# Every fourth expert slot of the first tile summed by POOL in SBUF instead of by PE

## The chip, the cores and the metric

The kernel runs on one core of a Trainium2 chip. The number is the device time of one execution in microseconds; the median of three runs of the kernel before is 1160.29 us (1155.86 to 1161.13). All arithmetic is in float32.

## The reference, cut to what matters

Two transformer blocks over 256 tokens of width 1024. The change touches one part of the second, the expert layer. For each token, 8 heads choose 16 of 16,384 experts each, so 128 experts a token. An expert is a row of `u` and a row of `v`, 1024 numbers each.

```
act = gelu(einsum('thkd,td->thk', u[expert], xt))      # one dot product a chosen expert
return einsum('thk,thkd->td', w * act, v[expert])      # weighted sum of the 128 rows of v
...
h = h + peer_ffn(rmsnorm_2(h, ffn_norm), ...)
gate = sigmoid(rmsnorm_2(h, ple_gate_norm) @ ple_gate_w)
h = h + (p @ ple_proj) * gate
```

## The kernel before

The 256 tokens are two tiles of 128, a token a partition. A slot is one chosen expert of every token of a tile: slots 0 to 127 belong to tile 0, 128 to 255 to tile 1. The expert part works slot after slot, and its order is written out by hand in the program of each engine.

POOL issues one gather a slot (L511). It brings 128 rows of 8 KB, the `u` and the `v` row of each token's expert, into a page of SBUF. Pages are old buffers under their old names: `ig`, `kT`, `spare`, `tail`, `xc_rg`, `gl`, `ga`, and from slot 35 on also `sm`. So there are seven pages for slots 0 to 27 and eight later, and a gather waits until the slot that had the page before is done (`slot_before`). The seventh slot before slot 10 is slot 3; slot 22 takes the page of 15, slot 30 that of 23.

DVE makes the dot product of the `u` half with the token's row (`dot`, L2038) and writes one number a token. Between dots it goes on choosing the experts of later heads, two steps a slot for 10 of 16 slots. ACT takes two slots at a time (`weigh`): gelu (L1406), times the probability (L1412), then for each slot a diagonal matrix of the weights (L1420, four buffers). PE multiplies that diagonal with the `v` half, 2 x 512 columns, and so adds the weighted rows to the sums in PSUM (`expert_sum`, L973). These sums started from the residual. When PE is done with a slot it raises `row_used`, for which POOL's gather waits.

In the first 52 slots of tile 0, PE, ACT and DVE also finish the attention and the mixing of tile 1's tokens between the slots (`second_tokens`; scores L721, turned weights L730, values L743, queries L922); DVE's L1750 and L1753 belong to it. From slot 52 on PE makes tile 1's queries. When tile 0's slots are summed, ACT copies the sums to `x3` (`tile_sums`, L1426), DVE makes their squares (L2045), PE turns them (L1074), DVE multiplies by a gain (`norm_out`, L1527), PE makes the gate (L1082), one product behind each slot of tile 1 (`first_gate`), and DVE adds the gated part (L2060). SP loads the weights of later stages into a ring of three slots.

Of the kernel before, what the change touches and what calls it, by code (L numbers as in the profile page):

```python
# [19 lines left out]
ALU = mybir.AluOpType  # L20
# [5 lines left out]
D = 1024  # L26
NT = SEQ // P
KC = D // P
HALF = 512
# [67 lines left out]
for _name, _width in COLS:  # L97
# [16 lines left out]
        "mixT_made", "mixed_full", "sums_copied", "sums_turned", "sums_gained", "rstd_made", "wp_used", "wo_full", "keys_loaded", "tok_full", "tok_moved", "query_turned", "query_moved",  # L114
        "pscore_full", "pscore_moved", "ple_moved",
        "choice_step", "top_shift", "top_exp", "chosen", "prob_made", "dot_made", "gelu_made", "w_made", "diag_made",
        "row_used", "sums_moved", "h2_made", "gate_full", "gate_moved", "y_made"]

# [2 lines left out]
BATCH = 2  # L123
DIAGS = 4
LAG = 32
TILE_SLOTS = PEER_HEADS * TOPK
SLOTS = NT * TILE_SLOTS
# [24 lines left out]
def slot_before(g):  # L152

    n = landing_of(g)
    return PAGE_SLOTS[page_of(g)][n - 2] if n > 1 else None

# [26 lines left out]
def two_blocks(nc, x, wall, cols, rows, lambdas, sub_keys, peer_uv, out):  # L185
    with ExitStack() as ctx:
# [231 lines left out]
        def _(pool):  # L418
# [76 lines left out]

            pool.wait_ge(s["intra_masked"], 2)

            for g in range(SLOTS):
                if g % TOPK == 0:
                    pool.wait_ge(s["chosen"], g // TOPK + 1)  # L500
                if g == 4:

                    pool.wait_ge(s["o_full"], NT)
                if g == 6:
                    pool.wait_ge(s["o_gated"], NT)
                if g == PAGE_SLOTS[7][0]:

                    pool.wait_ge(s["ao_full"], len(STEPS2))
                if slot_before(g) is not None:
                    pool.wait_ge(s["row_used"], slot_before(g) + 1)  # L510
                nc.gpsimd.indirect_dma_start(out=rows_uv[page_of(g)], out_offset=None, in_=peer_uv,  # L511
                                             in_offset=bass.IndirectOffsetOnAxis(ap=experts[:, g:g + 1], axis=0))\
                    .then_inc(row_here[page_of(g)], 16)
# [3 lines left out]
        def _(pe):  # L517
# [449 lines left out]
            att_turn(2)  # L967

            def expert_sum(g):
                t, n = g // TILE_SLOTS, g % DIAGS  # L970
                pe.wait_ge(s["diag_made"], g + 1)
                for c in range(2):
                    ins = nc.tensor.matmul(acc[t][:, c, :], diag[:, n * P:(n + 1) * P],  # L973
                                           rows_uv[page_of(g)][:, D + c * HALF:D + (c + 1) * HALF],
                                           start=False, stop=True, skip_group_check=True)
                ins.then_inc(s["row_used"], 1)
# [109 lines left out]

            def first_gate():

                for _ in range(4):
                    yield  # L1090
                pe.wait_ge(s["ple_moved"], 2)
                turn_sums(0)
                for _ in range(4):
                    yield
                pe.wait_ge(s["normed"], 2 * NT + 1)
                for c in range(2):
                    for k in range(KC):
                        embedding_gate(0, c, (k,))
                        yield

            for g in range(TILE_SLOTS):
                expert_sum(g)
                second_tokens(g)
            between = first_gate()
            for g in range(TILE_SLOTS, SLOTS):
# [9 lines left out]
        def _(act):  # L1115
# [285 lines left out]
            def weigh(b):  # L1401

                slots = range(b * BATCH, (b + 1) * BATCH)
                at = slots[0] % LAG
                act.wait_ge(s["dot_made"], slots[-1] + 1)
                nc.scalar.activation(acts[:, at:at + BATCH], dots[:, at:at + BATCH], ACT.Gelu_apprx_tanh)\  # L1406
                    .then_inc(s["gelu_made"], 1)
                if slots[0] % TOPK == 0:
                    act.wait_ge(s["prob_made"], slots[0] // TOPK + 1)
                act.wait_ge(s["gelu_made"], b + 1)  # L1410
                for g in slots:
                    ins = nc.scalar.activation(wk[:, g % LAG:g % LAG + 1], acts[:, g % LAG:g % LAG + 1], ACT.Copy,  # L1412
                                               scale=probs[:, g:g + 1])
                ins.then_inc(s["w_made"], 1)
                act.wait_ge(s["w_made"], b + 1)
                for g in slots:
                    if g >= DIAGS:
                        act.wait_ge(s["row_used"], g - DIAGS + 1)
                    n = g % DIAGS
                    nc.scalar.activation(diag[:, n * P:(n + 1) * P], ident[:, :], ACT.Copy,  # L1420
                                         scale=wk[:, g % LAG:g % LAG + 1]).then_inc(s["diag_made"], 1)

            def tile_sums(t):

                act.wait_ge(s["row_used"], (t + 1) * TILE_SLOTS)
                nc.scalar.activation(x3[:, t, :].rearrange("p (c n) -> p c n", c=2), acc[t], ACT.Copy)\  # L1426
                    .then_inc(s["h2_made"], 1)

# [19 lines left out]
            for b in range(SLOTS // BATCH):  # L1448
                weigh(b)
                last = (b + 1) * BATCH - 1  # L1450
                while head_at < NT * PEER_HEADS and dot_of_step((head_at - 1) * CHOICE_TURN + SHIFT_STEP) < last:
                    top_exp(head_at)
                    head_at += 1
                if last == 1:
                    att_move(2)
                    att_exps(3)
                if last == 3:
                    queries_moved(2)
                if last == 5:
                    att_move(3)  # L1460
                    scores_moved(2)
                if last == 17:
                    att_exps(4)
                if last == 21:
                    att_exps(5)
                    att_move(4)
                if last == 23:
                    tokens_moved(3)
                if last == 25:
                    att_move(5)  # L1470
                if last == 27:
                    queries_moved(3)
                if last == 29:
                    scores_moved(3)
                if last == 31:
                    sparse_std(1)
                if last == 49:
                    mixed_std(1)
                for n in range(4, len(QUERIES)):
                    first = 52 + 12 * (n - 4)  # L1480
                    if last == first + 9:
                        tokens_moved(n)
                    if last == first + 13:
                        queries_moved(n)
                    if last == first + 15:
                        scores_moved(n)
                if last == 123:
                    embeddings_moved(0)
                if last == 127:
                    embeddings_moved(1)  # L1490
                if last == TILE_SLOTS + 1:
                    tile_sums(0)
                if last == TILE_SLOTS + 3:
                    norm_std(6)
                if last == TILE_SLOTS + 33:
                    gate_moves(0)
            tile_sums(1)
            norm_std(7)
# [4 lines left out]
        def _(dve):  # L1503
# [572 lines left out]
            for g in range(SLOTS):  # L2076
                dot(g)
                for _ in range(choice_rate(g)):
                    next(between, None)
                if g == 0:  # L2080
                    att_biased(3)
                if g == 7:
                    att_out(2)
                if g == 9:
                    att_out(3)
                if g == 12:
                    mixed_gained(3, 1, 0, pa[:, HALF:2 * HALF])
                if g == 15:
                    att_biased(4)
                if g == 19:  # L2090
                    att_biased(5)
                if g == 26:
                    att_out(4)
                if g == 29:
                    att_out(5)
                if g == 30:
                    sparse_sums(1)
                if g == 33:
                    sparse_scaled(1)
                if g == 38:  # L2100
                    mixed_gained(4, 1, 4, pa[:, D:D + HALF])
                if g == 51:
                    rstd_made(1)
                if g == 54:
                    sums_gained(2)
                    sums_gained(3)
                if g == 56:
                    norm_gained(1)
                if g == TILE_SLOTS + 3:
                    gate_input(0)  # L2110
                if g == TILE_SLOTS + 5:
                    norm_out(6, col("gate_g", 0, KC), 0)
                if g == TILE_SLOTS + 7:
                    gate_scale(0)
                if g == TILE_SLOTS + 37:
                    dve.wait_ge(s["ple_moved"], 2)
                    gated(0)
            gate_input(1)
# [108 lines left out]
```

## Time and profile before

| what | value |
|---|---|
| median of three runs | 1160.29 us |
| profiled execution | 1158.14 us |
| its span | 1155.9 us |
| PE busy | 1019.4 us (88%) |
| DVE busy | 640.1 us (55%) |
| ACT busy | 403.1 us (35%) |
| POOL busy | 299.0 us (26%) |
| bytes moved | 349.29 MB |

The span runs from the first to the last instruction of one profiled execution; the time of that execution is 2.2 us more. In the rows, POOL's DMA_INDIRECT is the issue of a gather, not its transfer. A PE group "x4" of L973 is one slot: two products of 512 columns, each recorded as two. Slots have no number in the trace: the gathers stand in the order of the slots, so the n-th gather is that of slot n - 1. The part in square brackets is the idle time ahead of an instruction and what ended it.

### The profile page before, as it was taken

To read this page: it belongs to the slowest core of one execution; us is meant where nothing else is said; L and a number is where in the kernel's file an instruction comes from. 1 tells how busy PE (TensorE), PEld (TensorE's weight loads), DVE (VectorE), ACT (ScalarE), POOL (GpSimd) and SP (SyncE) were. 2 spreads that over 40 slices of the span, in tenths; PEclk is the share of its full clock that TensorE was granted. 3 is DMA by queue.
4 is the path that set the end of the run, shared out by engine and by line. 5 is a ranking of instruction groups with operands and counts; after the bars stand their busy time and mean duration, and the time that the engine had idled before them with its cause. 6 is when DMAs were issued, how large, how long until landed. Compare 5 with 4: busy or idle time off the path is not lost.

```text
span 1155.9 us, 9588 instructions
## 1 busy us (share of the span) xinstructions
PE 1019.4 (88%) x3171; PEld 540.5 (47%) x3171; DVE 640.1 (55%) x1470; ACT 403.1 (35%) x1042; POOL 299.0 (26%) x304
## 2 busy tenths in 40 slices
PE   6999989999999997978989898979799777777777
PEld 5887448644685454434434443434344222322223
DVE  2506245405443438677757575656776677667451
ACT  0133244311353235263343432424533332333222
POOL 3000000001000003334434332425446333443420
PEclk9999999999999998999999998989899999999999
DMA  7445424244624429989999999999999999999980
GB/s 282 147 146 218 145 73 146 73 145 164 219 82 157 171 81 421 412 296 365 412 416 422 423 422 421 421 422 422 411 403 414 422 422 420 422 421 422 422 366 19
DMA packets 43681, 349.29 MB, mean 302 GB/s; under 512 B 4880, under 2 KB 5008, under 8 KB 6128
## 3 DMA queue, kind: packets, MB, share of 16 engines
q0 software_dynamic: 37296, 269.89, 57.0%
q1 hardware_dynamic: 6336, 78.79, 17.9%
q8 instruction: 25, 0.41, 0.1%
q14 instruction: 24, 0.20, 0.0%
HBM read 347.35 MB, written 1.05 MB: 301 GB/s over the span
## 4 chain that ended last, share of the span: by engine, by line
PE 60%; DMA 24%; DVE 8%; ACT 5%; issue 2%; SPq 0%; POOL 0%; POOLq 0%; DVEq 0%; ACTq 0%
PE pp L973 20%; DMA tail<-in_peer_uv,small 10%; DMA kT<-in_peer_uv,small 10%; PE pp L546 7%; PE pp L570 4%; PE pp L574 4%; PE pp L556 3%; PE pp L1082 3%; PE pp L681 2%; PE pp L659 2%; PE pp L701 2%; PE pa L922 2%; DMA gl<-in_peer_uv,small 2%; PE pp L890 2%; DVE tail L2038 1%
## 5 line engine op out<-in xcount | busy, mean ns | idle before, releaser
L1406 ACT ACTIVATE small<-small 128x2 f32<-128x2 f32 x128 | 26.1, 204 | 386.4 <-DVE small L2038 386.1
L973 PE MATMUL pp<-ig,diag 128*128 128x512 f32 x132 | 68.1, 640 | 29.4 <-ACT diag L1420 29.4
L1420 ACT ACTIVATE diag<-ident,small 128x128 f32<-128x128 f32 x256 | 89.4, 394 | 5.2 <-PE pp L973 1.0
L973 PE MATMUL pp<-spare,diag 128*128 128x512 f32 x132 | 66.7, 629 | 26.4 <-ACT diag L1420 26.4
L546 PE MATMUL pp<-hT,ring 128*128 128x256 f32 x384 | 85.5, 386 | 3.2 <-DMA ring<-in_wall 3.2
L973 PE MATMUL pp<-xc_rg,diag 128*128 128x512 f32 x128 | 65.5, 636 | 24.5 <-ACT diag L1420 24.4
L973 PE MATMUL pp<-ga,diag 128*128 128x512 f32 x128 | 64.4, 627 | 24.0 <-ACT diag L1420 24.0
L546 PEld LDWEIGHTS pp<-hT,ring 128*128 128x128 f32 x384 | 74.4, 194 | 14.0 <-issue 3.6
L511 POOL DMA_INDIRECT ig<-in_peer_uv,small x33 | 35.2, 1066 | 140.6 <-DVE small L2025 70.3
L973 PE MATMUL pp<-kT,diag 128*128 128x512 f32 x132 | 63.9, 608 | 1.8 <-ACT diag L1420 1.8
L466 POOL IOTA tail<- 128x256 int32 x1 | 0.3, 342 | 248.6 <-DVE xs L1689 248.6
L973 PE MATMUL pp<-tail,diag 128*128 128x512 f32 x132 | 64.0, 608 | 0.0
L973 PE MATMUL pp<-gl,diag 128*128 128x512 f32 x128 | 61.5, 603 | 1.9 <-ACT diag L1420 1.9
L1412 ACT ACTIVATE small<-small 128x1 f32<-128x1 f32 x256 | 61.4, 286 | 5.1
L570 PE MATMUL pp<-ring,hT 128*128 128x512 f32 x128 | 60.8, 622 | 0.0
L574 PE MATMUL pp<-hT,ring 128*128 128x256 f32 x256 | 58.1, 381 | 0.0
L2038 DVE CUSTOM_DVE_ANT_0 kT<-kT,xc_rg 128x1024 f32<-128x1024 f32 x33 | 40.4, 1224 | 28.8 <-DMA kT<-in_peer_uv,small 28.8
L511 POOL DMA_INDIRECT xc_rg<-in_peer_uv,small x32 | 37.8, 1181 | 71.1 <-PE pp L973 70.5
L2038 DVE CUSTOM_DVE_ANT_0 ga<-ga,xc_rg 128x1024 f32<-128x1024 f32 x32 | 39.2, 1225 | 30.1 <-DMA ga<-in_peer_uv,small 30.0
L2038 DVE CUSTOM_DVE_ANT_0 ig<-ig,xc_rg 128x1024 f32<-128x1024 f32 x33 | 40.5, 1226 | 27.6 <-DMA ig<-in_peer_uv,small 27.6
L973 PEld LDWEIGHTS pp<-ig,diag 128*128 128x128 f32 x132 | 24.2, 196 | 65.3 <-ACT diag L1420 43.2
L973 PEld LDWEIGHTS pp<-spare,diag 128*128 128x128 f32 x132 | 23.9, 194 | 64.7 <-ACT diag L1420 44.2
(396 smaller groups left out, 1882.9 us busy)
## 6 DMA issues: line engine op xcount, KB each, us to landing
ring<-in_wall SPq DMA_DIRECT2D x36, 2048.0 KB, 7.8
xs<-in_x SPq DMA_DIRECT2D x2, 512.0 KB, 3.8
post_g<-in_rows POOLq DMA_DIRECT2D x2, 512.0 KB, 7.9
lt<-in_sub_keys SPq DMA_DIRECT2D x1, 1024.0 KB, 6.9
out<-xs SPq DMA_DIRECT2D x4, 256.0 KB, 4.8
ig<-in_peer_uv,small POOLq DMA_INDIRECT x33, 12.4
kT<-in_peer_uv,small POOLq DMA_INDIRECT x33, 12.6
spare<-in_peer_uv,small POOLq DMA_INDIRECT x33, 12.5
```

Of the source, the lines that this page charges most:

```text
L511: nc.gpsimd.indirect_dma_start(out=rows_uv[page_of(g)], out_offset=None, in_=peer_uv, in_offset=bass.IndirectOffsetOnAxis(ap=experts[:, g: ...
L546: ins = nc.tensor.matmul(buf[:, c, :], w[:, k, c * P:(c + 1) * P], h3[:, k, :], start=(k == 0), stop=(k == KC - 1))
L556: ins = nc.tensor.matmul(buf[:, t, 0:width], h3[:, k, t * P:(t + 1) * P], w[:, k, 0:width], start=(k == 0), stop=(k == KC - 1))
L570: ins = nc.tensor.matmul(buf[:, t, :], h3[:, k, t * P:(t + 1) * P], w[:, k, :], start=(k == 0), stop=(k == KC - 1))
L574: ins = nc.tensor.matmul(flat[:, c, :], w[:, k, c * P:(c + 1) * P], h3[:, k, :], start=(k == 0), stop=(k == KC - 1))
L659: ins = nc.tensor.matmul(bufs[c][:, t, :], gl3[:, k, t * P:(t + 1) * P], wo[c][:, k, :], start=(k == 0), stop=False)
L973: ins = nc.tensor.matmul(acc[t][:, c, :], diag[:, n * P:(n + 1) * P], rows_uv[page_of(g)][:, D + c * HALF:D + (c + 1) * HALF], start=False ...
L1082: ins = nc.tensor.matmul(acc[t][:, c, :], h3[:, k, t * P:(t + 1) * P], w[:, k, :], start=(k == 0), stop=(k == KC - 1))
L1406: nc.scalar.activation(acts[:, at:at + BATCH], dots[:, at:at + BATCH], ACT.Gelu_apprx_tanh)\
L1412: ins = nc.scalar.activation(wk[:, g % LAG:g % LAG + 1], acts[:, g % LAG:g % LAG + 1], ACT.Copy, scale=probs[:, g:g + 1])
L1420: nc.scalar.activation(diag[:, n * P:(n + 1) * P], ident[:, :], ACT.Copy, scale=wk[:, g % LAG:g % LAG + 1]).then_inc(s["diag_made"], 1)
L2038: V.tensor_tensor_reduce(out=row_u, in0=row_u, in1=xn[t], scale=1.0, scalar=0.0, op0=ALU.mult, op1=ALU.add, accum_out=dots[:, g % LAG:g % ...
```

## The change

In tile 0 the slots 3, 7, 11, ..., 127 (32 of 128, `by_pool`) get no diagonal from ACT and no product on PE. POOL sums them itself. Ahead of the gather that takes such a slot's page, it waits for the weight (`w_made`), multiplies the `v` half of the page by it, in place, and adds it to `x3[:, 0, :]`, a row of SBUF that is free then; the first of the 32 writes it directly. It waits for its own result before it issues the gather. The counters `row_used`, `diag_made` and the four diagonal buffers go by the slots that PE still sums (`PE_AT`). At the end PE adds POOL's row to the sums in PSUM by a product with the identity, behind slot 134 (`joined`), and what follows for tile 0 moves later: the copy of the sums from slot 129 to 137, the squares from 131 to 139, the turn of the sums from behind slot 132 to behind 140, the gain from 133 to 144, the move of the gate from 161 to 173, the gated sum from 165 to 177.

```diff
+def by_pool(g):
+    return g < TILE_SLOTS and g % 4 == 3
+PE_AT = [sum(not by_pool(h) for h in range(g)) for g in range(SLOTS + 1)]
+POOL_AT = [g - PE_AT[g] for g in range(SLOTS + 1)]
...
+            def pool_sum(g):
+                pool.wait_ge(s["w_made"], g // BATCH + 1)
+                row, w = rows_uv[page_of(g)][:, D:2 * D], wk[:, g % LAG:g % LAG + 1]
+                if POOL_AT[g] == 0:
+                    ins = nc.gpsimd.tensor_scalar(x3[:, 0, :], row, w, None, ALU.mult)
+                else:
+                    step(nc.gpsimd.tensor_scalar(row, row, w, None, ALU.mult))
+                    ins = nc.gpsimd.tensor_tensor(x3[:, 0, :], x3[:, 0, :], row, ALU.add)
+                ins.then_inc(s["pool_summed"], 1)
+                pool.wait_ge(s["pool_summed"], POOL_AT[g] + 1)
...
-                if slot_before(g) is not None:
-                    pool.wait_ge(s["row_used"], slot_before(g) + 1)
+                before = slot_before(g)
+                if before is not None and by_pool(before):
+                    pool_sum(before)
+                elif before is not None:
+                    pool.wait_ge(s["row_used"], PE_AT[before] + 1)
...
             def first_gate():
-                for _ in range(4):
+                for _ in range(6):
+                    yield
+                pe.wait_ge(s["pool_summed"], POOL_AT[SLOTS])
+                for c in range(2):
+                    ins = nc.tensor.matmul(acc[0][:, c, :], ident[:, :], x3[:, 0, c * HALF:(c + 1) * HALF],
+                                           start=False, stop=True, skip_group_check=True)
+                ins.then_inc(s["joined"], 1)
+                for _ in range(6):
                     yield
...
             for g in range(TILE_SLOTS):
-                expert_sum(g)
+                if not by_pool(g):
+                    expert_sum(g)
                 second_tokens(g)
...
                 for g in slots:
-                    if g >= DIAGS:
-                        act.wait_ge(s["row_used"], g - DIAGS + 1)
-                    n = g % DIAGS
+                    if by_pool(g):
+                        continue
+                    if PE_AT[g] >= DIAGS:
+                        act.wait_ge(s["row_used"], PE_AT[g] - DIAGS + 1)
+                    n = PE_AT[g] % DIAGS
...
             def tile_sums(t):
-                act.wait_ge(s["row_used"], (t + 1) * TILE_SLOTS)
+                if t == 0:
+                    act.wait_ge(s["joined"], 1)
+                else:
+                    act.wait_ge(s["row_used"], PE_AT[SLOTS])
...
-                if last == TILE_SLOTS + 1:
+                if last == TILE_SLOTS + 9:
                     tile_sums(0)
...
-                if g == TILE_SLOTS + 3:
+                if g == TILE_SLOTS + 11:
                     gate_input(0)
-                if g == TILE_SLOTS + 5:
+                if g == TILE_SLOTS + 16:
                     norm_out(6, col("gate_g", 0, KC), 0)
```

On POOL's queue, at the gathers of slots 19 to 23, `xc_rg` is the page of slot 18 and `kT` that of slot 15. Before:

```order
L511 DMA gl<-in_peer_uv,small 128x2048 [waits row_used]
L511 DMA ga<-in_peer_uv,small 128x2048 [waits row_used]
L511 DMA ig<-in_peer_uv,small 128x2048 [waits row_used]
L511 DMA kT<-in_peer_uv,small 128x2048 [waits row_used]
L511 DMA spare<-in_peer_uv,small 128x2048 [waits row_used]
```

After:

```order
L537 DMA gl<-in_peer_uv,small 128x2048 [waits row_used]
L537 DMA ga<-in_peer_uv,small 128x2048 [waits row_used]
L537 DMA ig<-in_peer_uv,small 128x2048 [waits row_used]
L516 TENSOR_SCALAR kT<-kT,small 128x1024 [waits w_made]
L517 TENSOR_TENSOR xs<-xs,kT 128x1024 [waits pool_step]
L537 DMA kT<-in_peer_uv,small 128x2048 [waits pool_summed]
L537 DMA spare<-in_peer_uv,small 128x2048 [waits row_used]
```

Two instructions now stand in front of the gather of slot 22, and everything behind it on POOL stands behind them too. `xs` is the buffer of `x3`.

On PE's queue, from slot 22 (`kT`) to slot 24 (`tail`), with the turned weights (`pa<-ident,sm`) and the values (`pa<-nq,sm`) of the attention between them. Before:

```order
L973 MATMUL pp<-kT,diag 128x512 [waits diag_made]
L973 MATMUL pp<-kT,diag 128x512
L730 MATMUL pa<-ident,sm 128x128 [waits att_exp]
L730 MATMUL pa<-ident,sm 128x128 x7
L973 MATMUL pp<-spare,diag 128x512 [waits diag_made]
L973 MATMUL pp<-spare,diag 128x512
L743 MATMUL pa<-nq,sm 128x64 [waits att_moved]
L743 MATMUL pa<-nq,sm 128x64 x3
L973 MATMUL pp<-tail,diag 128x512 [waits diag_made]
```

After:

```order
L999 MATMUL pp<-kT,diag 128x512 [waits diag_made]
L999 MATMUL pp<-kT,diag 128x512
L756 MATMUL pa<-ident,sm 128x128 [waits att_exp]
L756 MATMUL pa<-ident,sm 128x128 x7
L769 MATMUL pa<-nq,sm 128x64 [waits att_moved]
L769 MATMUL pa<-nq,sm 128x64 x3
L999 MATMUL pp<-tail,diag 128x512 [waits diag_made]
```

The two products of slot 23 (`spare`) are gone, and the attention's values and slot 24 move up by them.

## Rows read from the trace of the kernel before

**Rows 1.** The page: the span, and busy time (share of the span) and instructions of PE.
```profile
span 1155.9 us, 9588 instructions
...
PE 1019.4 (88%) x3171; PEld 540.5 (47%) x3171; DVE 640.1 (55%) x1470; ACT 403.1 (35%) x1042; POOL 299.0 (26%) x304
```
**Rows 2.** The page: GB/s in 40 slices of 28.9 us.
```profile
GB/s 282 147 146 218 145 73 146 73 145 164 219 82 157 171 81 421 412 296 365 412 416 422 423 422 421 421 422 422 411 403 414 422 422 420 422 421 422 422 366 19
```
**Rows 3.** Table by stretches: us, busy PE, PEld, DVE, ACT, POOL, PEclk, DMA, GB/s.
```profile
460.00:480.00 20.00, 19.78 (x73) 10.61 (x71) 14.07 (x33) 8.71 (x25) 7.95 (x9) 1.00 1.02 422
480.00:490.00 10.00, 9.57 (x25) 4.40 (x26) 6.92 (x23) 2.05 (x7) 3.95 (x4) 1.00 1.01 405
490.00:510.00 20.00, 15.48 (x42) 6.63 (x41) 16.83 (x46) 10.76 (x31) 6.04 (x6) 1.00 0.85 306
510.00:530.00 20.00, 16.89 (x70) 9.60 (x69) 9.73 (x23) 11.24 (x32) 8.70 (x7) 1.00 0.87 317
530.00:550.00 20.00, 17.23 (x53) 8.42 (x52) 17.50 (x52) 7.60 (x19) 9.02 (x8) 1.00 0.98 369
640.00:700.00 60.00, 51.84 (x128) 23.28 (x127) 34.73 (x85) 23.62 (x68) 22.80 (x22) 0.96 1.01 423
830.00:840.00 10.00, 10.00 (x18) 4.18 (x18) 5.99 (x10) 2.81 (x11) 3.83 (x3) 0.75 0.96 360
```
**Rows 4.** Line L511, the gathers: one page's issues, and issue to landing.
```profile
L511 POOL DMA_INDIRECT ig<-in_peer_uv,small x33: 932/938/1872, 430.5 to 1105.8; - x33
...
DMA to landing us min/median/max: 5.5/12.5/22.6
```
**Rows 5.** POOL in order of time, 488 to 537 us: start, us, what, idle before.
```profile
505.32 1.98 POOL L511 DMA_INDIRECT gl<-in_peer_uv,small  x1 [1.64 <-PE pp L973]
510.00 1.73 POOL L511 DMA_INDIRECT ga<-in_peer_uv,small  x1 [2.69 <-PE pp L973]
...
517.25 0.94 POOL L511 DMA_INDIRECT kT<-in_peer_uv,small  x1 [3.09 <-PE pp L973]
519.84 0.94 POOL L511 DMA_INDIRECT spare<-in_peer_uv,small  x1 [1.66 <-PE pp L973]
...
532.62 1.12 POOL L511 DMA_INDIRECT sm<-in_peer_uv,small  x1 [0.30 <-issue]
```
**Rows 6.** The chain of waits, 480 to 545 us: start, us, what.
```profile
489.60 1.23 DVE spare L2038
...
509.60 1.97 ACT sm L1260 x8
...
517.85 1.72 PE pp L973 x4
...
541.94 1.72 PE pp L973 x4
543.66 0.86 PE pp L867 x2
```
**Rows 7.** DVE in order of time, 508 to 513 us.
```profile
509.71 1.20 DVE L2038 CUSTOM_DVE_ANT_0 spare<-spare,xc_rg 128x1024 f32<-128x1024 f32 x1
```
**Rows 8.** Groups of instructions of POOL by form: count, busy us, mean ns.
```profile
L492 POOL TENSOR_SCALAR_AFFINE_SELECT gl<-gl 64x512 f32<-64x512 f32 x2 | 1.3, 654 | 41.0 <-ACT gl L1315 41.0
...
L467 POOL CAST mask<-tail 128x256 f32<-128x256 int32 x1 | 1.0, 964 | 0.1
L471 POOL MEMSET lt<- 128x1024 f32 x1 | 0.9, 945 | 0.0
```
**Rows 9.** The page: the group of the diagonals.
```profile
L1420 ACT ACTIVATE diag<-ident,small 128x128 f32<-128x128 f32 x256 | 89.4, 394 | 5.2 <-PE pp L973 1.0
```
**Rows 10.** All engines in order of time, 824 to 834 us.
```profile
824.43 1.23 DVE L1527 TENSOR_TENSOR hT<-pa,colt 128x1024 f32<-128x1024 f32 x1 [2.74 <-PE pa L1074]
...
833.71 0.94 POOL L511 DMA_INDIRECT spare<-in_peer_uv,small  x1 [5.98 <-PE pp L973]
```
**Rows 11.** POOL in order of time, 792 to 798 us.
```profile
794.43 1.60 POOL L511 DMA_INDIRECT xc_rg<-in_peer_uv,small  x1 [2.14 <-PE pp L973]
```
**Rows 12.** The chain of waits, 1100 us to the end.
```profile
1112.51 13.41 DMA tail<-in_peer_uv,small
```

More of the change, by code:

```diff
@@ L116 @@
         "choice_step", "top_shift", "top_exp", "chosen", "prob_made", "dot_made", "gelu_made", "w_made", "diag_made",
-        "row_used", "sums_moved", "h2_made", "gate_full", "gate_moved", "y_made"]
+        "row_used", "pool_summed", "joined", "sums_moved", "h2_made", "gate_full", "gate_moved", "y_made"]
 UPDATE_BANKS = (0, 1, 2)
@@ L969, in expert_sum @@
             def expert_sum(g):
-                t, n = g // TILE_SLOTS, g % DIAGS
-                pe.wait_ge(s["diag_made"], g + 1)
+                t, n = g // TILE_SLOTS, PE_AT[g] % DIAGS
+                pe.wait_ge(s["diag_made"], PE_AT[g] + 1)
                 for c in range(2):
@@ L1490, in _ @@
                     embeddings_moved(1)
-                if last == TILE_SLOTS + 1:
+                if last == TILE_SLOTS + 9:
                     tile_sums(0)
-                if last == TILE_SLOTS + 3:
+                if last == TILE_SLOTS + 13:
                     norm_std(6)
-                if last == TILE_SLOTS + 33:
+                if last == TILE_SLOTS + 45:
                     gate_moves(0)
@@ L2108, in _ @@
                     norm_gained(1)
-                if g == TILE_SLOTS + 3:
+                if g == TILE_SLOTS + 11:
                     gate_input(0)
-                if g == TILE_SLOTS + 5:
+                if g == TILE_SLOTS + 16:
                     norm_out(6, col("gate_g", 0, KC), 0)
-                if g == TILE_SLOTS + 7:
+                if g == TILE_SLOTS + 18:
                     gate_scale(0)
-                if g == TILE_SLOTS + 37:
+                if g == TILE_SLOTS + 49:
                     dve.wait_ge(s["ple_moved"], 2)
```

## The prediction

> **What bounds the kernel now.** I read the page first, then the table by stretches, the gathers' own line, and last the chain of waits. The page gives a span of 1155.9 us [rows 1]; the profiled execution took 1158.14 us, 2.2 us more than its span, and the median of the runs is 1160.29 us, 2.15 us above that execution. PE is busy for 88% of the span, which looks like the bound. The GB/s row says something else: from slice 16 of 40 to slice 38 all show 403 to 423 GB/s but the third and fourth of them, 296 and 365 [rows 2]. That is the expert part: 256 gathers, the first issued at 430.5 us [rows 4]. Each brings 128 rows of 8 KB, 1.049 MB, which at 421 GB/s (423 in the stretch of 640 to 700 us) is 2.49 us [rows 3]. 256 of them need 637 us whatever the engines do. So the question for any edit is whether the DMA queue always holds a gather. From issue to landing a gather takes 5.5 us at least and 12.5 us in the median [rows 4]. The difference, 7.0 us, is queueing: a gather may be issued 7 us later in the median case before the DMA runs dry.
>
> Where it does run dry is the stretch of 480 to 550 us. Against 421 GB/s the four stretches of it lack 0.4, 5.5, 4.9 and 2.5 us of transfer, as 20 x (421 - 306) / 421 = 5.5 for the second [rows 3]: 13.3 us together. After that only 830 to 840 shows one, 360 GB/s, 1.4 us [rows 3]. These 14.7 us are the prize; all else moves no end. In the dry stretch POOL issues a gather (0.94 us) and then waits for PE's sum of the slot that held the page [rows 5], and the chain of waits runs through PE, DVE and ACT in turn [rows 6]. In it stand the expert sums of slots 23, 27 and 31, three groups of four records, of which the first and the last are shown (517.85 and 541.94).
>
> **The change part by part.**
> Removed: of tile 0's 128 slots, 32 lose their matmuls, 1.72 us each (541.94) [rows 6], 55 us of PE, and their diagonal, 0.39 us each [rows 9], 12.6 us of ACT. In the saturated 640 to 700 us all of it lies beside the DMA and is worth nothing.
>
> Added on POOL: 32 times a weighting and 31 times a sum over 128x1024. No row shows either operation, so I bound them. One stream: the memset of the same size took 0.945 us; the affine select of 64x512 took 654 ns, 1.28 ns an element, 1.31 us for 1024; the slowest rate is the cast, 964 ns for 256, which would be 3.9 us [rows 8]. I take 1.2 us for the weighting, nearest to the first two, with ends of 0.95 and 3.9. The sum reads two streams; I take twice as much, 2.4 us, with ends of 0.95 and 7.7. Together S = 3.6 us a slot, ends 1.9 and 11.6. The Trainium skill, page "GPSIMD Engine Reference", section "Elementwise — side-by-side cycle accounting", gives 4497 ns for a POOL tensor_tensor add of 2048 fp32; half of it is an estimate of 2.25 us, and the total would be 0.15 us lower by it. No row here shows it.
>
> POOL's queue: behind the sum stand its gather and all that follow, since POOL works in order; DVE waits for those pages. Four back-to-back gathers take four times 1.25 us (0.94 plus a gap of 0.30), 5.0 us [rows 5]. With S that is 8.6 us for four slots, and the DMA needs 9.96. POOL keeps up while S stays under 5.0 us. The page's weight is ready sooner than PE's sum was, so the gather behind it is issued about S after the gather before, where it used to come 2.6 us after (517.25 to 519.84) [rows 5]: 2 to 3 us late at most, inside the 7.0 us of queueing. Saturated part of tile 0: 0 us.
>
> DVE beside POOL: the gather at 510.00 us took 1.73 us, not 0.94 [rows 5]. A dot (L2038, two inputs in SBUF) ran from 509.71 to 510.91 [rows 7]. The gather at 505.32 took 1.98 us, the one at 519.84 only 0.94 [rows 5]. So POOL waits for the end of a two-input DVE instruction. Whether DVE waits for POOL in turn, these rows can't show, since a gather reads only one index a partition. I bound that hold from both sides: nothing, or the whole S of 3.6 us for each slot. The Trainium skill, page "SBUF — State Buffer", section "Who interferes with whom", says that it works both ways: a DVE instruction with two SBUF inputs and a POOL instruction that reads SBUF exclude each other, and the first to start holds the read port to its end. That speaks against the change, and the second rival is what it would do here; the half of it that this trace can show, it agrees with (1.73 against 0.94 us). In my sum: a dot takes 1.23 of every 2.49 us, so about half of the POOL instructions meet one, and where DVE is on the chain I charge half of the 2.4 us of a sum, 1.2 us. In 640 to 700 us DVE is busy 34.73 of 60 us [rows 3], 5.8 of 10; with all of S it is 9.4 of 10, still free.
>
> Moved: tile 0's end. Before, DVE stands at the turned sums for 2.74 us (824.43), POOL's next gather then waits for 5.98 us [rows 10], and 830 to 840 us has the 1.4 us deficit. The copy of the sums moves 8 slots later, DVE's squares 8, its L1527 instruction 11, ACT's gate move 12, the gated sum 12. DVE then meets turned sums four slots after PE made them, so the wait goes; what is late there is only PE, whose gate products add 0.86 us (two records, as at 543.66) [rows 6] to a slot of 1.72, 2.58 against 2.49, as before. The join adds two matmuls, 1.72 us of PE once. At slot 134 all POOL sums are long done (that of slot 127 stands in front of gather 135, issued 12 us before its landing), so its wait is empty. No instruction of SP moves. Worth: 1 us of the 1.4, which the join about eats where PE is busy 10.00 of 10 us (830 to 840) [rows 3]: I count 0.5 us of gain. If the wait were late instead, DVE and the gathers behind it would pay it in full, up to the 5.98 us seen now less 5 us of queueing. From the landing of the last gather (1112.51 + 13.41) [rows 12] on, 30 us, nothing changes.
>
> The dry stretch, which decides. Gain: slots 23, 27 and 31 leave the chain, 3 x 1.72 = 5.2 us. Slots 3, 7 and 11 come before it; PE is busy 19.78 of 20 us there (460 to 480) [rows 3], yet no dot starts before its page has landed, so of their 5.2 us I keep 2.1: 7.3 us in all. Against it, (a) DVE is itself on the chain from 489 to 507 us (busy 16.83 of 20), where the sums of slots 15 and 19 fall: 2 x 1.2 = 2.4 us; (b) the gathers behind sums. Gather 29 was issued at 517.25; 2.1 us earlier it is at 515.1; then 1.25 us, S = 3.6, and gather 30 goes out at 520.0, where before it did at 519.84. So one gather in four gains nothing and the next are bunched behind it. I take half of the 4.9 us left as lost, 2.4. Net gain 2.5 us.
>
> Sum: -2.5 (dry stretch), -0.5 (tile end), 0 elsewhere: -3.0 us. On the profiled execution 1158.14 - 3.0 = 1155.1; on the runs' median 1160.29 - 3.0 = 1157.3 us, which is my number.
>
> **The rivals.**
> First, the cheap case (faster): S near 2.2 us and DVE hardly held. Then (a) and (b) vanish, 7.3 us are gained in the dry stretch and 1.4 at the tile's end: 1160.3 - 8.7 = 1151.6 us. For it: POOL idles between gathers, and the best end of the bounds is 1.9. Against: chain pieces removed from one engine seldom all count, as DVE and ACT stand between them [rows 6]. The whole prize, 14.7 us, would be 1145.6.
>
> Second, DVE becomes the bound of the dry stretch (slower). Its busy time in 480 to 550 us is 6.9 + 16.8 + 9.7 + 17.5 = 51 us of 70 [rows 3]. Six sums fall there. Let each hold DVE for all of S, 3.6 us: 21.6 us. The idle 19 of 70 us, 27%, take 5.8 us of it, and 7.3 us are gained on the chain: 21.6 - 5.8 - 7.3 = +8.5 us, 1168.8. It decides from a hold of 7.3 / (6 x 0.73) = 1.7 us a slot. For it: the lock seen above [rows 5, 7], and DVE's 16.83 and 17.50 of 20 us. Against: a hold costs only when a dot is due just as POOL sums, and nothing where DVE waits for PE anyway, as for the 2.74 us [rows 10].
>
> Third, POOL itself too slow (slower): tile 0's 128 gathers go from 430.5 to 794.43 us, where the 129th is issued [rows 4, 11], 11.4 us for four, other loads included. So S over 6.4 us makes POOL the bound of the whole tile; at S = 7 it is 0.6 x 32 = 19 us, 1179. It needs nearly the cast's rate.
>
> That the sums aren't made by POOL is no rival: the order above shows them on its queue, and no longer on PE's.
>
> **How the numbers follow.** Forecast, within 5.8 us (0.5%, about what a measurement can tell) of before: 0.51. First rival 0.24; second 0.18; third 0.07. The forecast's own range is 1154 to 1164. To leave out no more than 2 in 10 the range goes from 1149 (past the first rival) to 1169 (the second). Faster by over 0.5% 0.24, within 0.51, slower 0.25.
>
> **What would show it.** POOL's L516 near 1.2 us and L517 near 2.4 us, longer when a dot runs. The interval from gather to gather behind a sum near 1.25 + S. GB/s of 420 and more from 560 us on; less anywhere in 560 to 820 refutes the 0 us. Deficits in the dry stretch of 10 to 11 us, not 13.3. DVE dots of 1.23 us with new gaps ahead of them while L517 runs, or longer dots, if the lock works both ways. Near 830 us no DVE wait before L1566, which is L1527 of before. I am wrong if the dry stretch nearly closes, or if it spreads past 560 us.

## The result: 1210.93 us, 52.5 us slower, and the profile after

The changed kernel takes 1210.93 us in the median (1209.67 to 1213.89, 4 runs) against 1158.41 us of the kernel before beside it; the ratio is 1.0459, 95% interval 1.0435 to 1.0483. I had forecast 1157.3 and a range to 1169.

The page of the profiled execution, span, busy time and GB/s in 40 slices of 30.2 us:

```profile
span 1207.8 us, 9370 instructions
...
PE 1003.9 (83%) x3047; PEld 528.8 (44%) x3047; DVE 704.2 (58%) x1470; ACT 392.9 (33%) x1010; POOL 493.0 (41%) x367
...
GB/s 270 147 132 209 139 139 71 139 140 165 153 196 105 81 356 384 225 212 339 367 424 372 357 371 398 337 395 385 346 412 421 421 421 423 420 422 421 422 410 20
```

PE is busy 15.5 us less, ACT 10.2, and POOL 194 us more [rows 1]. The saturation is gone: counted from 1, of the slices 17 to 30, past the end of tile 0, only one reaches 421 GB/s and twelve stay below 400; before, only two of the slices from 16 on fell below 400 before the last two [rows 2]. Tile 1 moves at 420 GB/s and more from slice 31 on, as it did.

The table by stretches, same columns as [rows 3]:

```profile
480.00:550.00 70.00, 47.45 (x139) 23.75 (x139) 48.71 (x98) 23.70 (x67) 42.46 (x25) 0.83 0.67 242
550.00:860.00 310.00, 230.57 (x502) 97.81 (x501) 225.18 (x452) 96.85 (x275) 262.15 (x148) 0.86 0.95 374
```

Before, the same two stretches of the clock read:

```profile
480.00:550.00 70.00, 59.17 (x184) 29.05 (x185) 50.98 (x142) 31.65 (x87) 27.71 (x24) 1.00 0.91 341
550.00:860.00 310.00, 278.08 (x669) 123.65 (x668) 201.86 (x503) 117.75 (x340) 125.55 (x112) 0.95 1.01 418
```

Transfer missing against before: 70 x (341 - 242) / 421 = 16.5 us in the dry stretch and 310 x (418 - 374) / 421 = 32.4 us in the stretch for which I had written 0 us. It has spread past 560 us, which I had named as a sign of being wrong. POOL is busy 85% of the latter. POOL in order of time, two rounds of four slots:

```profile
655.24 1.67 POOL L537 DMA_INDIRECT sm<-in_peer_uv,small  x1 [0.27 <-POOL xs L517]
657.23 1.89 POOL L537 DMA_INDIRECT ig<-in_peer_uv,small  x1 [0.31 <-issue]
659.42 1.68 POOL L537 DMA_INDIRECT kT<-in_peer_uv,small  x1 [0.30 <-issue]
661.40 0.94 POOL L537 DMA_INDIRECT spare<-in_peer_uv,small  x1 [0.30 <-issue]
662.38 3.00 POOL L516 TENSOR_SCALAR tail<-tail,small 128x1024 f32<-128x1024 f32 x1
665.46 2.36 POOL L517 TENSOR_TENSOR xs<-xs,tail 128x1024 f32<-128x1024 f32 x1
668.09 1.14 POOL L537 DMA_INDIRECT tail<-in_peer_uv,small  x1 [0.27 <-POOL xs L517]
...
674.15 2.86 POOL L516 TENSOR_SCALAR sm<-sm,small 128x1024 f32<-128x1024 f32 x1
677.09 2.35 POOL L517 TENSOR_TENSOR xs<-xs,sm 128x1024 f32<-128x1024 f32 x1
679.71 1.68 POOL L537 DMA_INDIRECT sm<-in_peer_uv,small  x1 [0.27 <-POOL xs L517]
```

From 655.24 to 679.71 are eight gathers, 12.2 us for four. There is no wait for PE in these rows; every gap is 0.3 us. They are typical: from 568.8 to 870.4 us stand 24 such rounds of four gathers, 12.6 us in the mean (11.1 to 17.3), and in 15 of them POOL waited for no other engine; in the others it waited for PE as well. I had 8.6 us. The sum (L517, 2.35 us) is what I took, 2.4. The weighting (L516) took 2.86 us where I had 1.2. And the gathers, 0.94 us each when nothing is in the way, took 1.67, 1.89 and 1.68 us.

What is in the way is DVE. Of the 96 gathers issued between 550 and 850 us, 47 took over 1.3 us, and 43 of these began while a dot of DVE ran. DVE's dots, of the same moments:

```profile
664.28 1.23 DVE L2077 CUSTOM_DVE_ANT_0 ig<-ig,xc_rg 128x1024 f32<-128x1024 f32 x1 [0.46 <-DMA ig<-in_peer_uv,small]
...
673.94 2.41 DVE L2077 CUSTOM_DVE_ANT_0 tail<-tail,xc_rg 128x1024 f32<-128x1024 f32 x1 [1.15 <-DMA tail<-in_peer_uv,small]
...
677.47 3.04 DVE L2077 CUSTOM_DVE_ANT_0 xc_rg<-xc_rg 128x1024 f32<-128x1024 f32 x1 [0.43 <-DMA xc_rg<-in_peer_uv,small]
```

The dot at 677.47 began 0.38 us after the sum at 677.09 and ended at 680.51, 1.07 us behind the sum's end (679.44), though it needs only 1.23 us: it stood still as long as POOL summed (such a standstill is called a hold below). In this trace 22 dots began while an L517 ran. 19 of them ended 1.08 to 1.09 us behind it. Two began within 0.01 us of it; they took 1.22 us, and it was the sum that stood still, 3.43 us. The last began 0.05 us before the sum's end. The gather at 679.71 then met the dot just set free and took 1.68 us: one hold makes the next. The dot at 673.94 met the weighting (674.15) and ended 2.20 us after the weighting's start, long before its end: the weighting holds a dot too, but only through its first 1.1 us or so. Dots that began later into an L516 took 1.22 us. In the mean a dot of tile 0 takes 1.53 us now, and took 1.22 before. Not only dots are held: the 128x512 tensor_tensor of the expert choice that began at 665.64 us, inside a sum, took 2.72 us, where its median is 0.69.

### The profile page after: what moved, and what is told of

It reads as the page before. It is cut to its first block, busy times and chain, and to the rows that moved or that the text cites. A ratio compares the mean times of both kernels' runs of the same rounds, so it can differ in the third digit from the quotient of the medians.

```text
span 1207.8 us, 9370 instructions
## 1 busy us (share of the span) xinstructions
PE 1003.9 (83%) x3047; PEld 528.8 (44%) x3047; DVE 704.2 (58%) x1470; ACT 392.9 (33%) x1010; POOL 493.0 (41%) x367
## 3 DMA queue, kind: packets, MB, share of 16 engines
q1 hardware_dynamic: 6336, 78.79, 17.2%
## 4 chain that ended last, share of the span: by engine, by line
PE 47%; DMA 23%; POOL 14%; DVE 9%; ACT 4%; issue 3%; SPq 0%; POOLq 0%; DVEq 0%; ACTq 0%
DMA tail<-in_peer_uv,small 13%; PE pp L999 12%; PE pp L572 7%; PE pp L596 4%; PE pp L600 4%; POOL xs L517 3%; PE pp L582 3%; DMA kT<-in_peer_uv,small 2%; PE pp L1108 2%; PE pp L707 2%; PE pp L685 2%; PE pp L727 2%; POOL sm L516 2%; DMA sm<-in_peer_uv,small 2%; POOL tail L516 2%
## 5 line engine op out<-in xcount | busy, mean ns | idle before, releaser
L1440 ACT ACTIVATE small<-small 128x2 f32<-128x2 f32 x128 | 26.1, 204 | 456.5 <-DVE small L2077 456.5
L999 PE MATMUL pp<-spare,diag 128*128 128x512 f32 x128 | 72.9, 698 | 53.0 <-ACT diag L1456 52.9
L999 PE MATMUL pp<-ig,diag 128*128 128x512 f32 x128 | 71.0, 682 | 36.4 <-ACT diag L1456 36.4
L999 PE MATMUL pp<-ga,diag 128*128 128x512 f32 x124 | 68.8, 683 | 36.6 <-ACT diag L1456 36.4
L537 POOL DMA_INDIRECT ig<-in_peer_uv,small x33 | 39.7, 1202 | 112.0 <-DVE small L2064 70.3
L1456 ACT ACTIVATE diag<-ident,small 128x128 f32<-128x128 f32 x224 | 79.4, 395 | 4.2
L2077 DVE CUSTOM_DVE_ANT_0 tail<-tail,xc_rg 128x1024 f32<-128x1024 f32 x33 | 48.2, 1462 | 34.2 <-DMA tail<-in_peer_uv,small 34.1
L2077 DVE CUSTOM_DVE_ANT_0 ig<-ig,xc_rg 128x1024 f32<-128x1024 f32 x33 | 48.6, 1474 | 23.6 <-DMA ig<-in_peer_uv,small 23.5
L2077 DVE CUSTOM_DVE_ANT_0 xc_rg<-xc_rg 128x1024 f32<-128x1024 f32 x32 | 46.1, 1440 | 22.1 <-DMA xc_rg<-in_peer_uv,small 22.1
L2077 DVE CUSTOM_DVE_ANT_0 sm<-sm,xc_rg 128x1024 f32<-128x1024 f32 x28 | 41.0, 1464 | 28.9 <-DMA sm<-in_peer_uv,small 28.8
L999 PEld LDWEIGHTS pp<-ga,diag 128*128 128x128 f32 x124 | 24.3, 211 | 74.9 <-ACT diag L1456 53.0
```

What stands on the lines that cost most here:

```text
L2077: V.tensor_tensor_reduce(out=row_u, in0=row_u, in1=xn[t], scale=1.0, scalar=0.0, op0=ALU.mult, op1=ALU.add, accum_out=dots[:, g % LAG:g % ...
```

## The experiments

Each kernel was timed against the kernel before on the same chip as itself (there 1158.05 to 1158.21 us).

**The change without POOL's arithmetic.**

```diff
-                    step(nc.gpsimd.tensor_scalar(row, row, w, None, ALU.mult))
-                    ins = nc.gpsimd.tensor_tensor(x3[:, 0, :], x3[:, 0, :], row, ALU.add)
...
+                ins = nc.gpsimd.memset(x3[:, 0, 0:1], 0.0) if POOL_AT[g] else nc.gpsimd.memset(x3[:, 0, :], 0.0)
```

> The changed kernel, but POOL writes one element where it weighted and summed a page, so the output lacks the 32 slots; what PE and ACT no longer do, the order of the gathers and the moved tile end stay. Theory A (POOL's time in front of the gathers): the loss of 52 us goes and the removal alone shows, 1150 to 1158 us. Theory B (DVE held by POOL's reads): the same. Theory C (something else in the change costs, the moved tile end or the page order): it stays over 1170 us. If the chain really was worth 7.3 us, 1151 us.

Measured 1158.42 us, ratio 1.0006 (0.9989 to 1.0023). The whole loss is POOL's arithmetic. It also shows that what PE and ACT no longer do gains nothing that can be told. Three stretches of this trace hint at where my 7.3 us went:

```profile
480.00:490.00 10.00, 10.00 (x20) 4.45 (x20) 3.88 (x14) 1.08 (x4) 2.64 (x3) 0.72 0.88 347
490.00:500.00 10.00, 5.72 (x11) 2.29 (x10) 8.36 (x26) 6.13 (x16) 2.90 (x4) 0.83 0.71 259
510.00:520.00 10.00, 9.18 (x20) 4.69 (x21) 7.04 (x18) 8.15 (x22) 2.16 (x2) 0.69 0.61 208
```

PE's granted clock is 0.69 to 0.83 here, a mix of the two levels 1.2 and 2.4 GHz, where in the trace of before it was 1.00 in every row of 460 to 550 us [rows 3]. On PE in order of time, one slot after a wait of 3.95 us:

```profile
510.19 3.78 PE L994 MATMUL pp<-ga,diag 128*128 128x512 f32 x4 [3.95 <-ACT diag L1451]
```

3.78 us instead of 1.72 to 1.98: PE had idled for 3.95 us, and the slot behind the wait ran at the lower level. But that needs no removed work. The kernel below that keeps all of PE's work and only moves tile 0's end has such a slot too, and in 480 to 550 us it moves 326 GB/s where this one moves 327 (first PE in order of time, then the row of the table):

```profile
497.22 3.78 PE L973 MATMUL pp<-tail,diag 128*128 128x512 f32 x4
...
480.00:550.00 70.00, 59.34 (x173) 28.38 (x172) 47.98 (x130) 30.38 (x84) 22.39 (x21) 0.93 0.86 326
```

So single slots of one trace don't show what the removal did. The runs together do: the mean granted clock is 0.953 to 0.962 in the ten runs of this kernel, 0.969 to 0.979 in the 13 of before beside them, and 0.973 to 0.983 in the twelve runs of the one with the moved end. PE is busy 982.7 us here, only 36.7 less than before, though 55 us of products are gone and 1.7 us of the join are new: what stays takes some 17 us longer. That this is why the gain is missing isn't shown, since no run held the clock up with the work away.

**Where in tile 0.** POOL takes its slots only up to 47, or only from 51 on.

```diff
-    return g < TILE_SLOTS and g % 4 == 3
+    return g < 48 and g % 4 == 3                  # the first run
+    return 48 <= g < TILE_SLOTS and g % 4 == 3    # the second
```

> POOL takes every fourth slot only up to slot 47, the stretch where the DMA ran dry: 12 of the 32. The transfer lost there in the changed kernel is about 32 us more than before. Theory A, with an empty queue that passes every delay on: +30 us, 1188. If each POOL slot cost the same (52/32 = 1.6 us): +20 us, 1178.

> POOL takes every fourth slot only from 51 to 127: 20 of the 32, where the DMA was saturated before. My step said 0 us here. Theory A: four slots take POOL 12.2 us against 11.4 us that the tile gave, +15 to +20 us, 1176. If the whole loss came from the dry stretch: 1158.

Measured 1182.53 us (1.0203, 1.0175 to 1.0231), 24.5 us for 12 slots, and 1184.19 us (1.0214, 1.0181 to 1.0246), 26.1 us for 20. Together 50.6 of the 52.5 us; the first lies between my two numbers, the second above mine. The first run moves 422 GB/s again in 600 to 820 us, the second 380:

```profile
600.00:820.00 220.00, 186.79 (x457) 82.82 (x456) 139.88 (x340) 80.58 (x234) 96.91 (x81) 0.95 1.01 422
```

```profile
600.00:820.00 220.00, 162.99 (x361) 70.32 (x362) 156.36 (x305) 67.21 (x198) 184.43 (x103) 0.85 0.96 380
```

An early slot costs 2.0 us, a late one 1.3; the loss is in both halves, and the second is the one my sum denied. Its size follows from the gathers: those of slots 58 to 128 came every 11.4 us for four before (199.4 us for the 70), 12.8 in the changed kernel (224.8) and 12.9 in this second run (225.8). The last is 26.4 us more than before, near the 26.1 that the run lost.

**POOL's time without its reads.** Five memsets of 128x1024 in place of the two instructions, 4.9 us a slot, writes only.

```diff
-                    step(nc.gpsimd.tensor_scalar(row, row, w, None, ALU.mult))
-                    ins = nc.gpsimd.tensor_tensor(x3[:, 0, :], x3[:, 0, :], row, ALU.add)
...
+                for _ in range(4 if POOL_AT[g] else 2):
+                    step(nc.gpsimd.memset(x3[:, 0, :], 0.0))
+                ins = nc.gpsimd.memset(x3[:, 0, :], 0.0)
```

> As the changed kernel, but POOL spends about as long per slot (five memsets of 128x1024, about 5 us) only writing, never reading SBUF; the output lacks the 32 slots' rows. Theory A (time on the gather queue): most of the loss stays, 1200 us or more. Theory B (POOL's reads hold DVE's dots): dots fall back to 1.22 us and most of the loss goes, under 1180 us.

Measured 1175.24 us, ratio 1.0136 (1.0108 to 1.0164): 17.2 us. POOL in order of time, from one slot's memsets to the next:

```profile
660.28 0.95 POOL L534 DMA_INDIRECT sm<-in_peer_uv,small  x1 [0.27 <-POOL xs L514]
661.53 1.11 POOL L534 DMA_INDIRECT ig<-in_peer_uv,small  x1 [0.30 <-issue]
662.94 0.94 POOL L534 DMA_INDIRECT kT<-in_peer_uv,small  x1 [0.31 <-issue]
664.19 0.94 POOL L534 DMA_INDIRECT spare<-in_peer_uv,small  x1 [0.30 <-issue]
665.12 4.00 POOL L513 MEMSET xs<- 128x1024 f32 x4
```

Four slots take 10.1 us here, near the DMA's 9.96, and the gathers are short again; over 24 rounds behind 550 us it is 11.7 us in the mean (9.95 to 19.3), waits for PE in it. (The traced execution took 1180.15 us, 4.9 more than the median.) The dots on one buffer (DVE, 430 to 870 us: count, busy us, mean ns, idle before), in this kernel and in the changed one:

```profile
L2074 DVE CUSTOM_DVE_ANT_0 tail<-tail,xc_rg 128x1024 f32<-128x1024 f32 x19 | 23.3, 1224 | 10.3 <-DMA tail<-in_peer_uv,small 10.1
```

```profile
L2077 DVE CUSTOM_DVE_ANT_0 tail<-tail,xc_rg 128x1024 f32<-128x1024 f32 x17 | 28.6, 1685 | 24.2 <-DMA tail<-in_peer_uv,small 24.1
```

1.22 us against 1.69. Both theories hold a part: about a third of the loss comes by POOL's time in front of its gathers alone, and the other 35 us only with the reads (and with the 0.3 us a slot that this run is shorter).

**A POOL slot of half the length, with and without reads.** In one kernel ACT weights the page and POOL only adds it; in the other POOL writes for 2.4 us.

```diff
+                            nc.scalar.activation(row, row, ACT.Copy, scale=wk[:, g % LAG:g % LAG + 1])\
+                                .then_inc(s["row_weighed"], 1)
...
-                    step(nc.gpsimd.tensor_scalar(row, row, w, None, ALU.mult))
+                    pool.wait_ge(s["row_weighed"], POOL_AT[g])
```

```diff
+                if POOL_AT[g]:
+                    step(nc.gpsimd.memset(x3[:, 0, :], 0.0))
+                    step(nc.gpsimd.memset(x3[:, 0, 0:HALF], 0.0))
+                ins = nc.gpsimd.memset(x3[:, 0, :], 0.0)
```

> The change, but ACT weights the page (one 128x1024 activation, about 1 us) and POOL only adds it: POOL's time per slot falls from 5.5 to 2.6 us and its reads hold DVE for 2.34 us instead of 5.2. Four slots then take POOL about 8.5 us, under 9.96. Theory A plus B: the later stretch costs nothing, the early one some 8 us: 1158 to 1170. If only the number of interruptions counts and not their length: over 1180.

> As the write-only run, but about 2.4 us a slot (two memsets of 1024 columns and one of 512) instead of 4.9, so POOL's time in front of a gather is that of the run in which ACT weights, without a read of SBUF; the output lacks the 32 slots. If POOL's time alone made that run's +21 us: 1179. If its reads did (dots held by POOL, gathers held by dots): 1158 to 1164, and the difference is the price of the reads.

With reads 1179.10 us (1.0177, 1.0158 to 1.0196), 20.9 us; without 1160.59 (1.0020, 1.0005 to 1.0035), 2.4 us. At about the same time of POOL, the reads, with ACT's weighting beside them, cost 18.5 us more. By stretches the loss with reads is early: 480 to 550 us is as dry as in the change, the rest keeps 412 GB/s:

```profile
480.00:550.00 70.00, 50.23 (x134) 24.07 (x133) 43.48 (x93) 27.74 (x71) 29.37 (x22) 0.78 0.67 239
550.00:860.00 310.00, 241.04 (x556) 104.04 (x556) 241.97 (x498) 133.14 (x330) 209.34 (x137) 0.90 1.00 412
```

I had 1158 to 1170 for it and was wrong by 9 us. ACT's weighting takes 1.13 us a page, but no such instruction is on the chain of waits of 480 to 550 us. A dot held for 3.47 us (481.51) is, and so are five expert sums at the lower level, under a granted clock of 0.63 to 0.84 in the six rows of 480 to 540 us:

```profile
486.23 3.78 PE pp L999 x4
...
492.01 3.71 PE pp L999 x4
...
507.11 3.78 PE pp L999 x4
...
512.89 3.57 PE pp L999 x4
...
527.52 3.78 PE pp L999 x4
```

The chain of before has no expert sum over 2 us in that stretch, that of the writing kernel two. So in the dry stretch a hold may cost more than its own length, as PE idles meanwhile and comes back slower. But the kernel without POOL's arithmetic has four such sums on its chain (2.96 to 3.78 us) and loses nothing; how the 20.9 us divide between holds, clock and ACT's work isn't measured.

**PE and ACT keep everything.** The kernel before, tile 0's end moved, and POOL's work added.

```diff
+                if before is not None and before < TILE_SLOTS and before % 4 == 3:
+                    pool.wait_ge(s["w_made"], before // BATCH + 1)
+                    row, w = rows_uv[page_of(before)][:, D:2 * D], wk[:, before % LAG:before % LAG + 1]
+                    step(nc.gpsimd.tensor_scalar(x3[:, 0, :], row, w, None, ALU.mult))
+                    if before > 3:
+                        step(nc.gpsimd.tensor_tensor(x3[:, 0, :], x3[:, 0, :], row, ALU.add))
+                if before is not None:
+                    pool.wait_ge(s["row_used"], before + 1)
```

> As above, and POOL weights and sums the 32 slots as in the change (writing its product to the row of x3 instead of the page, the sum unused), while PE and ACT keep all 128 slots. Theory: what PE lost was worth nothing, so this costs what the change costs, 1205 to 1215 us. If the removed PE work was worth the 7.3 us of my sum, 1216 to 1220.

Measured 1211.02 us (1.0459, 1.0440 to 1.0478), the changed kernel's time to 0.1 us. From the other side: 55 us of PE and 12.6 us of ACT were worth nothing beside POOL's work.

**Tile 0's end alone moved.**

```diff
-                for _ in range(4):
+                for _ in range(12):
...
-                if g == TILE_SLOTS + 5:
+                if g == TILE_SLOTS + 16:
                     norm_out(6, col("gate_g", 0, KC), 0)
...
```

> The kernel before with nothing but tile 0's end moved as in the change (copy, squares, turn, gain, gate and gated sum later by 8 to 12 slots); POOL sums nothing. My step said -1 us for the move without the join. If the wait that goes was never late: 0. If the move costs (the gate later, the page order): +2 us or more, and that would be part of the 52.

Measured 1160.79 us, 1.0012 (0.9996 to 1.0028): no difference that can be told. The deficit at 830 us does go:

```profile
830.00:840.00 10.00, 7.40 (x16) 2.88 (x16) 5.24 (x9) 3.70 (x12) 4.08 (x4) 1.00 1.01 422
```

422 GB/s there, 360 before [rows 3]. In the runs' times a gain of 1.4 us isn't seen.

**Every eighth slot.**

```diff
-    return g < TILE_SLOTS and g % 4 == 3
+    return g < TILE_SLOTS and g % 8 == 3
```

> POOL takes every eighth slot of tile 0, 16 instead of 32. If each slot costs the same (52/32 = 1.6 us): +26, 1184. If the later stretch is a threshold (POOL's cycle over the DMA's), it costs nothing there, and the early stretch half of its 24: +12, 1170.

Measured 1177.73 us (1.0163, 1.0144 to 1.0183), 19.5 us for 16 slots, 1.2 us each against 1.6. It lies between my two numbers: 550 to 860 us moves 402 GB/s, so a single POOL slot in eight still costs later on, though the mean cycle of POOL is under the DMA's.

**The weighting.** By a constant; as a tensor_tensor with the weight broadcast; and both instructions in four pieces.

```diff
-                    step(nc.gpsimd.tensor_scalar(row, row, w, None, ALU.mult))
+                    step(nc.gpsimd.tensor_scalar(row, row, 0.01, None, ALU.mult))                   # first
+                    step(nc.gpsimd.tensor_tensor(row, row, w.broadcast_to([P, D]), ALU.mult))       # second
```

```diff
+                    for c in range(4):
+                        q = slice(c * 256, (c + 1) * 256)
+                        step(nc.gpsimd.tensor_scalar(row[:, q], row[:, q], w, None, ALU.mult))
+                        ins = nc.gpsimd.tensor_tensor(x3[:, 0, q], x3[:, 0, q], row[:, q], ALU.add)
```

> The change with the weighting by a constant instead of the weight a token; the output is off by the weights. If the 2.86 us of POOL's weighting come from the operand per partition, it falls to about 1.2 us, my term, and the time to about 1185 to 1190 us. If any one-input POOL arithmetic of this size takes 2.86 us, nothing moves: 1211.

> The change with the weighting as a tensor_tensor product with the weight broadcast over the columns. If POOL's time goes by streams it takes more than 2.86 us and the time rises over 1211. If a tensor_tensor of 1024 columns takes 2.34 us whatever it reads, 0.5 us less a slot: 32 x 0.5 = 16 us less at most, 1195 to 1205.

> The change with each weighting and sum cut into four pieces of 256 columns, so that a DVE dot waits for a piece and not for the whole. If the length of a hold is what costs: dots shorten to under 1.35 us in the mean and the time falls under 1211 in spite of about 1 us more of POOL overhead. If POOL's total time on the gather queue counts: longer, 1220 to 1245 us.

By a constant the weighting takes 2.80 to 2.84 us (means of two pages) and the time is 1210.80 (1.0436, 1.0403 to 1.0468): the operand a partition is not what costs. As a tensor_tensor it takes 1.94 us, a third less, yet the time falls by 2.5 us only, to 1208.48 (1.0436, 1.0418 to 1.0454), above the 1195 to 1205 that I gave for a shorter one. This product holds dots to its very end, as the sum does, and the sums behind it grow to 3.0 us in the mean: they wait for the dots just set free. In pieces the time is 1269.01 us (1.0981, 1.0936 to 1.1025) and over the range I gave. POOL in order of time, the first two pieces of one slot:

```profile
663.69 0.95 POOL L518 TENSOR_SCALAR sm<-sm,small 128x256 f32<-128x256 f32 x1
664.73 0.72 POOL L519 TENSOR_TENSOR xs<-xs,sm 128x256 f32<-128x256 f32 x1
665.43 0.93 POOL L518 TENSOR_SCALAR sm<-sm,small 128x256 f32<-128x256 f32 x1
666.43 1.26 POOL L519 TENSOR_TENSOR xs<-xs,sm 128x256 f32<-128x256 f32 x1
```

A quarter costs 0.95 and 0.72 us, four of each 6.7 us and not 5.2, and in this slot a dot slips in before each of the other three quarter sums, which then take 1.26 to 1.52 us; in other slots it meets quarter weightings too (24 of 124 took about 1.9 us). The slot grows from 5.6 to 9.3 us (663.69 to the next gather at 672.96), and four slots to 14.2 us (gathers at 658.72 and 672.96). The dots do get shorter, 1.31 us in the mean against 1.53, as the lock's theory wants; yet the time rises by another 58 us, with 324 GB/s in 550 to 860 us against 374. So shorter holds of DVE don't make up for a longer time of POOL in front of its gathers; part of that time, 9.3 - 6.7 = 2.6 us of this slot, is itself POOL waiting for dots and the gaps between pieces.

## Why the prediction was wrong

**POOL's queue is the step that failed.** I had S = 3.6 us and four gathers of 1.25: 8.6 us for four slots against the DMA's 9.96, so 0 us in the saturated part. Measured: 12.2 us. The sum was right (2.35 for 2.4 us; 2.25 was my estimate from the figure of the Trainium skill, page "GPSIMD Engine Reference", section "Elementwise — side-by-side cycle accounting", and the trace agrees with it to 0.1 us). The weighting was 2.86 us for 1.2: I took it by the memset and the affine select, and it lies toward the cast's end of my bounds [rows 8]. With the gaps S is 5.6 us on average (662.38 to 668.09 and 674.15 to 679.71), 2.0 more. The other 1.6 us are the four gathers, 6.6 us instead of 5.0, as dots stand before them; I had seen that in [rows 5] and did not put it into the cycle. My own threshold was S = 5.0 us, and S is over it. It was a strict one: 9.96 us is four gathers alone, and with the other loads the DMA gave four every 11.4 us. 12.8 us instead of 11.4 for four, over 70 slots, make 25 us, and the run by halves lost 26.1 us in the saturated part, where I wrote 0.

**Dry stretch.** I had 2.5 us of gain; the first 12 slots cost 24.5 us. Of the parts, (a) charged two holds of 1.2 us and (b) 2.4 us for gathers behind sums. A hold lasts up to a whole sum, and POOL's longer slot delays every gather behind it. Over the whole kernel the reads are worth at most 18 us at a short slot (ACT's weighting is in that) and 35 us at the long one (where POOL's slot is also 0.3 us longer). How the 24.5 us of the first 12 slots divide between holds and queue, no run shows.

**The gain of the chain, 7.3 us,** is nothing: without POOL's arithmetic the time is 1158.42 us. The step took durations of removed instructions for time of the chain. The granted clock of those runs is lower (0.953 to 0.962 against 0.969 to 0.979), so that what stays on PE is slower; that it is the whole reason isn't shown.

**What was right.** Work taken off PE and ACT in the saturated part is worth nothing (the kernel that keeps it all: 1211.02 us). Tile 0's end: the deficit at 830 us closes when it alone is moved, and the 0.5 us I gave it is too little to be told from nothing. In the changed kernel, whose tile 0 ends later, the same stretch shows 339 GB/s, with POOL busy 8.73 of 10 us.

**The rivals.** The second, the lock, named the mechanism and set the upper edge of my range, 1168.8; it assumed a free POOL and six slots. The third, POOL too slow, said it decides from S = 6.4 us, with gathers of 1.25. I wrote that this needs nearly the cast's rate; with a sum at twice the weighting it needs a weighting of 6.4 / 3 = 2.1 us, little over half of the cast's 3.9. With the four gathers at 6.6 us it decides from 11.4 - 6.6 = 4.8 us, and S was above. I gave it 0.07 by asking how likely S itself was, while the bounds I had written (1.9 to 11.6) reach well past it; the range to 1169 did not take them in. The two rivals are one in fact: the lock lengthens POOL's cycle and DVE's dots together.

## What to carry to other kernels

An engine that issues gathers from its queue is part of the transfer path: its idle share says little, and the number to compare with the DMA's time is its whole cycle, arithmetic plus gathers at the length they have when the other engine runs beside them. Arithmetic on POOL has to be priced instruction by instruction, and beside two-input work on DVE an instruction that reads SBUF is charged twice, once for itself and once for what it holds. Work taken from an engine that isn't the bound was worth nothing here though PE was busy for 88% of the span, and went with a lower granted clock of what is left.

## What the runs showed of the hardware that I had not expected

- On POOL a TENSOR_SCALAR of 128x1024 fp32 takes 2.86 us, with a constant 2.80 to 2.84; a TENSOR_TENSOR of two full inputs takes 2.34 us, one with its second input broadcast along the row 1.94 us. The operation with less to read is the slowest.
- At 128x256 they take 0.92 to 0.95 and 0.72 us. So four pieces cost more than one whole: 3.7 for 2.86 us of the weighting, 2.9 for 2.34 us of the sum, and gaps of about 0.1 us beside.
- A POOL sum stops a DVE dot wholly (3.04 us instead of 1.23), as the Trainium skill, page "SBUF — State Buffer", section "Who interferes with whom", says of two instructions that share the port, and the trace agrees. In two points the traces differ from it. The weighting, though it reads SBUF for 2.86 us, holds a dot only for its first 1.1 us. And the one that began first isn't always the one that goes on: where ACT weights, nine dots that began 0.03 to 0.55 us before a sum still ended 1.09 us behind it, while three that began 0.74 to 0.82 us before took 1.22 us and the sum waited.
- Memsets of POOL hold no dot: 1.23 us in the mean beside them, over all of tile 0.
